# A two-block transformer on one core: queue orders of the second mixer, tile 1's last copy at a feed-forward's end, and the output in halves

## The reference, cut to what matters

```python
def swiglu_2(h, w_in, w_out):
    g, u = jnp.split(h @ w_in, 2, axis=-1)
    return (jax.nn.silu(g) * u) @ w_out

def token_mixer(h, ...):                       # second block
    aq, ak, av, mq, mk, mv, mo, mg = jnp.split(h @ w_in, cuts, axis=-1)
    attn_out = merge_heads(dilated_attention_mixture(rotary(aq) * 64 ** -0.5, rotary(ak), av))   # 8 heads of 64
    qk = jax.nn.silu(conv5(concat([mq, mk])) + conv_b)      # 5 taps along the tokens, each channel for itself
    mq, mk = jnp.split(qk, 2, axis=-1)                      # 4 heads of 128
    mk = mk * 128 ** -0.5
    gates = mg + gate_bias
    cell = mlstm(mq, mk, mv, gates[0], gates[1]) + flip(mlstm(flip(mq), flip(mk), ...))   # two directions
    # in each: num / maximum(abs(den), exp(-m)), num and den linear in mk
    cell = cell * rsqrt(mean(cell ** 2) + eps)
    mlstm_out = sigmoid(mo) * (merge_heads(cell) * mlstm_norm_gain)
    return concat([attn_out, mlstm_out]) @ w_out

# second block: x = x + factor * rms_norm(h, gain) after each part
```

## Time and profile before

| | us |
|---|---|
| median of 3 runs (lowest to highest) | 2189.46 (2186.26 to 2193.22) |
| the three runs | 2189.46, 2186.26, 2193.22 |
| the profiled execution's own time | 2188.38 |
| its span, first to last instruction | 2186.6 |
| mean granted TensorE clock | 0.997 of full speed |

### The profile page before, as it was taken

One profiled execution on the slowest core, in us unless ns is written; L12 is line 12 of the kernel. 1 busy time (PEld: TensorE's weight loads), 2 busy tenths in 40 slices (PEclk: granted clock), 3 DMA queues, 4 the chain that ended last, 5 costly groups with the idle time before them and its releaser, 6 DMA issues.

```text
span 2186.6 us, 27850 instructions
## 1 busy us (share of the span) xinstructions
PE 2150.4 (98%) x10882; PEld 1807.2 (83%) x10882; DVE 1314.8 (60%) x1826; ACT 1070.1 (49%) x1540; POOL 70.9 (3%) x107
## 2 busy tenths in 40 slices
PE   8999999999999999999999999999999999999998
PEld 7888999888888899988878888778888888867887
DVE  5556866555655676655575566575556556667554
ACT  6444544444444454444454456544445445654443
POOL 0000010000000001000000000010000000001000
PEclk9999999999999999999999999999999999999999
DMA  7766654666666675476666656336666666534663
GB/s 244 236 185 185 204 180 139 218 192 186 199 188 188 180 211 178 137 230 187 188 195 191 185 163 188 99 101 216 191 187 199 187 188 177 164 98 144 186 188 99
DMA packets 313654, 393.65 MB, mean 180 GB/s; under 512 B 17796, under 2 KB 272020, under 8 KB 313524
## 3 DMA queue, kind: packets, MB, share of 16 engines
q1 hardware_dynamic: 308832, 375.52, 56.9%
q0 software_dynamic: 4528, 16.29, 2.4%
q10 hardware_dynamic: 164, 0.06, 0.0%
HBM read 390.75 MB, written 1.05 MB: 179 GB/s over the span
## 4 chain that ended last, share of the span: by engine, by line
PE 91%; DVE 3%; ACT 2%; issue 2%; DMA 1%; POOL 0%; SPq 0%; POOLq 0%; DVEq 0%; ACTq 0%
PE bank L307 25%; PE bank L309 24%; PE bank L308 24%; PE bank L301 4%; PE bank L303 4%; PE bank L302 4%; PE bank L433 2%; DMA stage<-in_mix_w_in 1%; ACT w_hi L284 1%; PE bank L446 1%; DVE w_lo L291 1%; PE bank L1375 1%; PE bank L909 1%; PE bank L1396 1%; DVE scratch L1807 0%
## 5 line engine op out<-in xcount | busy, mean ns | idle before, releaser
L291 DVE TENSOR_TENSOR w_lo<-stage,w_hi 128x1024 fp32r<-128x1024 f32 x711 | 865.7, 1224 | 666.1 <-ACT w_hi L284 665.1
L284 ACT ACTIVATE w_hi<-stage 128x1024 fp32r<-128x1024 f32 x711 | 748.4, 1059 | 727.3 <-PE bank L309 585.5
L307 PE MATMUL bank<-w_hi,xt_hi 128*128 128x512 f32 x1760 | 699.9, 398 | 3.7 <-DVE scratch L1718 3.1
L309 PE MATMUL bank<-w_hi,xt_lo 128*128 128x512 f32 x1760 | 687.2, 390 | 0.0
L308 PE MATMUL bank<-w_lo,xt_hi 128*128 128x512 f32 x1760 | 686.1, 390 | 0.0
L307 PEld LDWEIGHTS bank<-w_hi,xt_hi 128*128 128x128 f32 x1760 | 330.9, 188 | 73.2 <-DVE scratch L1718 3.9
L309 PEld LDWEIGHTS bank<-w_hi,xt_lo 128*128 128x128 f32 x1760 | 330.6, 188 | 70.8
L308 PEld LDWEIGHTS bank<-w_lo,xt_hi 128*128 128x128 f32 x1760 | 331.3, 188 | 64.4
L307 PE MATMUL bank<-w_hi,mt_hi 128*128 128x512 f32 x768 | 304.1, 396 | 4.0 <-DVE mt_lo L1865 1.9
L309 PE MATMUL bank<-w_hi,mt_lo 128*128 128x512 f32 x768 | 299.8, 390 | 0.0
L308 PE MATMUL bank<-w_lo,mt_hi 128*128 128x512 f32 x768 | 299.0, 389 | 0.0
(11 more groups left out here) (264 smaller groups left out, 1422.4 us busy)
## 6 DMA issues: line engine op xcount, KB each, us to landing
stage<-in_ffn_w SPq DMA_DIRECT2D x352, 256.0 KB, 3.3
stage<-in_ffn_w_in SPq DMA_DIRECT2D x352, 256.0 KB, 3.2
stage<-in_ffn_w SPq DMA_DIRECT2D x88, 512.0 KB, 3.6
stage<-in_ffn_w_out SPq DMA_DIRECT2D x88, 512.0 KB, 3.6
stage<-in_w_in SPq DMA_DIRECT2D x80, 512.0 KB, 4.4
stage<-in_mix_w_in SPq DMA_DIRECT2D x56, 512.0 KB, 4.2
stage<-in_w_out SPq DMA_DIRECT2D x16, 512.0 KB, 4.5
stage<-in_mix_w_out SPq DMA_DIRECT2D x16, 512.0 KB, 3.4
```

The costliest lines, as they stand in the source:

```text
L284: act.activation(w_hi[:, u % RING, :], stage[:, u % STAGED, :], ACT.Copy).then_inc(S["hi_ready"], 1)
L291: dve.tensor_tensor(w_lo[:, u % RING, :], stage[:, u % STAGED, :], f32(w_hi[:, u % RING, :]), ALU.subtract).then_inc(S["lo_ready"], 1)
L307: pe.matmul(o, m_hi, hi, start=first, stop=False)
L309: return pe.matmul(o, m_lo, hi, start=False, stop=last)
```

## The change

Seven edits.

1. End of an FFN: ACT's `act_h` of tile 1's last values comes ahead of `hi_upto(b + n + 5)`.
2. Mixer 2, gates: ACT's `hi_upto(b + 18)` comes behind the copy of g_feat.
3. Mixer 2, convolution: `conv_in(3)` in DVE's list for head 4 in place of head 5.
4. Mixer 2, Silu: ACT does it, and then the copy g_cols, ahead of `hi_upto(b + 36)` instead of behind. The scaling of the keys is left out; DVE multiplies g_em (the floor of the denominator) by 128 ** 0.5 instead, and m_pair(0) waits for the Silu itself.
5. Head loop, ACT: at h = 0 the exponentials come ahead of `hi_upto(b + 38)`, later the roundings come behind the squares.
6. Head loop, DVE: the order args, gated_cells(h - 2), cells(h - 1), weights(h) becomes args, weights(h), cells(h - 1), gated_cells(h - 2).
7. Output: the last stage's update of x in two halves of 512 columns for each tile, and four transfers of 256 KB in place of two of 512 KB.

```diff
@@ -541,8 +541,8 @@
                         act_h(act, s, 1, i)
             act_norm_sq(act, s, 0)
             act_silu(act, s, 1, STEPS - 1)
+            act_h(act, s, 1, STEPS - 1)
             hi_upto(act, b + n + 5)
-            act_h(act, s, 1, STEPS - 1)
             if s + 1 < len(STAGES):
                 hi_upto(act, b + n + 6)
                 act_xt(act, s + 1, 0)
@@ -609,7 +609,9 @@
         def x_at(s, t, h):
-            return 4 * s + 2 * t + h + 1 if s < BLOCK2 else 4 * BLOCK2 + 2 * (s - BLOCK2) + t + 1
+            if s < BLOCK2:
+                return 4 * s + 2 * t + h + 1
+            return 4 * BLOCK2 + 2 * (s - BLOCK2) + (t if s + 1 < len(STAGES) else 2 * t + h) + 1
         def x_done(s, t):
             return x_at(s, t, 1)
@@ -710,8 +712,10 @@
             else:
                 dve.wait_ge(S["post_scaled"], 2 * post_at(s, t))
                 dve.wait_ge(S["post_rstd"], post_at(s, t))
-                dve.scalar_tensor_tensor(x[:, t, :], r[:, t, :], rstd[:, t:t + 1], x[:, t, :], ALU.mult, ALU.add)\
-                   .then_inc(S["x_ready"], 1)
+                w = D if s + 1 < len(STAGES) else D // 2
+                for c in range(0, D, w):
+                    dve.scalar_tensor_tensor(x[:, t, c:c + w], r[:, t, c:c + w], rstd[:, t:t + 1], x[:, t, c:c + w],
+                                             ALU.mult, ALU.add).then_inc(S["x_ready"], 1)
         def act_pre_sq(act, s, t):
             act.wait_ge(S["x_ready"], x_done(s - 1, t))
@@ -1442,7 +1446,7 @@
                 if h == 0:
                     pe.wait_ge(S["mo_out"], at("mo_out", L, 2))
-                    pe.wait_ge(S["k_scaled"], at("k_scaled", L))
+                    pe.wait_ge(S["conv_silu"], at("conv_silu", L))
                 else:
                     pe_hold(pe, S["m_p"], at("m_p", L, 4 * h))
                 for j in range(NT):
@@ -1536,10 +1540,10 @@
             hi_upto(act, b + 17)
             act.wait_ge(S["used"], b + 8)
             aqk_tile(1)
-            hi_upto(act, b + 18)
             act.activation(half2, scale2[:, :], ACT.Copy, scale=0.5).then_inc(S["srow_out"], 1)
             act.wait_ge(S["gates"], at("gates", L))
             act.activation(g_feat, bank[0:NG, 2, 0:T], ACT.Copy).then_inc(S["gates_out"], 1)
+            hi_upto(act, b + 18)
             act.wait_ge(S["srow"], at("srow", L))
             act.activation(s_row, bank[:, 3, 0:T], ACT.Copy).then_inc(S["srow_out"], 1)
             hi_upto(act, b + 19)
@@ -1578,12 +1582,12 @@
                            .then_inc(S["a_exp"], 1)
                     if h in (1, 2, 4, 5):
                         conv_first((0, 0, 1, 1, 2, 3)[h])
-            hi_upto(act, b + 36)
+            act.wait_ge(S["conv"], at("conv", L))
+            act.activation(conv_y[:, :, :], conv_y[:, :, :], ACT.Silu).then_inc(S["conv_silu"], 1)
             act.wait_ge(S["g_cols_turned"], at("g_cols_turned", L))
             act.activation(g_cols, bank[:, 0, 0:64].rearrange("p (m d i r) -> p m d i r", m=2, d=2, i=NT), ACT.Copy)\
                .then_inc(S["g_cols"], 1)
-            act.wait_ge(S["conv"], at("conv", L))
-            act.activation(conv_y[:, :, :], conv_y[:, :, :], ACT.Silu).then_inc(S["conv_silu"], 1)
+            hi_upto(act, b + 36)
             def mvo_tile(t):
                 act.activation(va[:, t, :, 0:P], group[:, t, 0:512].rearrange("p (h e) -> p h e", h=H), ACT.Identity,
@@ -1616,13 +1620,15 @@
                                    accum_out=ss[:, 2 * h + i:2 * h + i + 1]).then_inc(S["m_ss"], 1)
             for h in range(H):
-                hi_upto(act, b + 38 + h)
                 for d in range(2):
                     act.wait_ge(S["m_arg"], at("m_arg", L, 4 * h + 2 * d + 2))
                     act.activation(m_w[:, d, :], m_e[:, d, :], ACT.Exp).then_inc(S["m_exp"], 1)
+                if h == 0:
+                    hi_upto(act, b + 38)
                 if h:
                     forward(h - 1)
                     squares(h - 1)
+                    hi_upto(act, b + 38 + h)
             forward(H - 1)
             act.wait_ge(S["mg_turned"], at("mg_turned", L, 2))
             act.activation(mt_hi[:, 4:6, :], merged[:, 0:2, :], ACT.Copy).then_inc(S["m_hi"], 1)
@@ -1752,8 +1758,8 @@
                 if h == 4:
                     conv_in(2)
                     conv_taps(1, (3, 4))
+                    conv_in(3)
                 if h == 5:
-                    conv_in(3)
                     conv_taps(2, (1, 2))
                 if h == 6:
                     conv_taps(2, (3, 4))
@@ -1771,9 +1777,6 @@
                                         bank[:, 2 + i, :].rearrange("p (h c) -> p h c", h=AH),
                                         a_rs[:, :, i:i + 1].broadcast_to([P, AH, DH]), ALU.mult)
             ins.then_inc(S["a_out"], 1)
-            dve.wait_ge(S["conv_silu"], at("conv_silu", L))
-            dve.tensor_scalar(conv_y[:, 4:8, :], conv_y[:, 4:8, :], float(P) ** -0.5, None, ALU.mult)\
-               .then_inc(S["k_scaled"], 1)
             lo_upto(dve, base + 36)
             for t in range(NT):
                 dve.wait_ge(S["m_hi"], at("m_hi", L, t + 1))
@@ -1845,12 +1848,14 @@
             dve.scalar_tensor_tensor(gm, gm, 1.0, rows[:, 1, 0:512].unsqueeze(1).broadcast_to([P, NT, 512]),
                                      ALU.add, ALU.mult).then_inc(S["mo_gain"], 1)
             dve.wait_ge(S["g_em"], at("g_em", L))
+            dve.tensor_scalar(g_em, g_em, float(P) ** 0.5, None, ALU.mult).then_inc(S["k_scaled"], 1)
+            dve.wait_ge(S["k_scaled"], at("k_scaled", L))
             for h in range(1, H):
                 args(h)
+                weights(h)
+                cells(h - 1)
                 if h >= 2:
                     gated_cells(h - 2)
-                cells(h - 1)
-                weights(h)
                 cell_var(h - 1)
                 lo_upto(dve, base + 36 + h)
             gated_cells(H - 2)
@@ -1906,9 +1911,11 @@
                 else:
                     sp_ffn(sp, s, A["ffn_w_in_2"][L, j], A["ffn_w_out_2"][L, j])
             for t in range(NT):
-                sp.wait_ge(S["x_ready"], x_done(len(STAGES) - 1, t))
-                sp.dma_start(out[0, t * P:(t + 1) * P, :], x[:, t, :]).then_inc(S["x_out"], 16)
-            sp.wait_ge(S["x_out"], 32)
+                for h in range(2):
+                    c = slice(h * 512, (h + 1) * 512)
+                    sp.wait_ge(S["x_ready"], x_at(len(STAGES) - 1, t, h))
+                    sp.dma_start(out[0, t * P:(t + 1) * P, c], x[:, t, c]).then_inc(S["x_out"], 16)
+            sp.wait_ge(S["x_out"], 64)
         @block.gpsimd
         def _(pool):
```

## The result

The changed kernel takes 2169.8 (median of 4 runs, 2169.18 to 2171.8) against 2188.39 for the kernel before on the same chip (4 runs, 2186.26 to 2193.22). The ratio is 0.9914, 95% interval 0.9898 to 0.9929: 0.9% faster. Forecast were 2174 and a range of 2170 to 2181, so the direction was right and the time lies 0.2 under the range (run once more beside later experiments, the same kernel took 2170.18, e9). The profiled execution took 2169.18 where that of before took 2188.38, and the spans differ by the same 19.2. The sum in the prediction was 14.9. The question is where the other 4.3 come from.

What follows compares the result with a forecast made beforehand. It took PE, busy 98%, as the bound, leaving stream gaps, granted clock and the tail. Terms of 1.1, 3.1, 0.3, 2.4, 3.2, 1.8, 2.7 and 0.3 summed to 14.9 off 2188.4; with 1.1 for a median, 2174, range 2170 to 2181.

Steps and rivals of the forecast that it cites:

- What bounds the kernel: Whole span: PE is busy 98%, so only gaps in its stream, its granted clock and the tail can move the time.
- Gates, conv, Silu: Second mixer: removed PE waits give 1.1 (gates), 3.1 (conv_in(3) earlier) and net 0.3 (Silu first, new wait 0.5 a layer).
- Exponentials ahead of two roundings: Second mixer's head loop: six m_pair waits of 5.6 go, new lateness loses 3.2, net gain 2.4 (0 to 4.5).
- rival B: Head loop: weights(0) still late, so the idle, the low clock and some overlap stay lost: 2181; chance 0.10.
- DVE becomes the slower of the two: Head loop: DVE needs 6.7 a head against PE's 6.3, part of a loss of 1.6 per layer.
- DVE late: Head loop: two heads leave DVE 0.8 late, so m_out(3) waits 2.4 in all.
- 0.16 a gap: PE's stream: each wait also loses 0.16 of matmul overlap; 17 gaps fewer give 2.7 (0 to 3.5).
- The clock: Layer 0's second mixer: the 1.2 GHz stretch behind the idle 2.10 at m_pair(1) goes, gaining 3.2.
- Rival A: Second mixer: idle of 2.4 and 1.8 before L1478 brings new low-clock stretches: one gives 2177, two 2180; chance 0.25.
- C: Rival, slower: the Silu ahead of the roundings starves PE at n = 30, giving 2177 to 2196; chance 0.03.
- D: Rival, no change: the gaps turn out hidden by other waits of the same length, 2186; chance 0.05.
- Output: Kernel's end: last update and stores in halves gain 0.3 (between -0.5 and +0.8).

Runs made afterwards that it cites:

- e9: The changed kernel, unedited, run again beside e6 and e7: 2170.18 (4 runs), ratio 0.9911.
- e5: The changed kernel with one more DVE product, its result unused, behind the w_lo of heads 1 and 2: 2172.72 (one run).
- e3: The changed kernel with DVE's old head-loop order back (gated cells and cells ahead of weights): 2171.86, ratio 0.9917.
- e1: The kernel before with the FFN edit alone (tile 1's last turned values copied ahead of the two roundings): 2185.53 against 2191.44, ratio 0.9977.
- e2: The changed kernel with head 0's two roundings ahead of the exponentials again: 2176.52, ratio 0.9942.
- e10: The kernel before with only head 0's exponentials moved ahead of the two roundings: 2181.94, ratio 0.996.
- e11: The kernel before with the conv edit alone (conv_in(3) one head earlier): 2185.09 against 2191.73, ratio 0.9977.
- e7: The changed kernel with e6's edit, w_lo up to b+34 moved behind the attention output, and head 2's denominators ahead of weights(3): 2166.16, ratio 0.989.
- e6: The changed kernel with the head loop's last DVE w_lo moved behind gated_cells(3): 2168.22, ratio 0.9901.

## Why the prediction was right, and where it was not

*What bounds the kernel.* Right: of the 19.2, all but the 0.5 at the end are gaps in PE's stream or its granted clock, and they lie at the waits in the earlier trace rows.

*Gates, conv, Silu.* Right in mechanism and nearly in size: 1.3, 3.7 and 0.8 (1.9 less 1.1) against 1.4, 3.4 and 0.3. conv alone on before gives the same as in the whole. The gates edit was neither tried alone nor undone; its 1.3 is read from the wait that went. The new wait of L1442 is 0.4 a layer, not 0.5, so the load and the Silu are the 3.2 that I gave them: in after too the Silu starts 1.30 behind the load's start. The Trainium skill, ScalarE: Activation LUTs, section "What ACT_TABLE_LOAD costs", has a drain of about 1.4 behind the load; as an estimate from it L1442 would wait 1.4 longer. The trace disagrees: it waits 0.40.

*Exponentials ahead of two roundings.* Right for m_pair(1), (2), (3): 6.5 against 6.6 with the overlap. The margin of 0.1 to 0.2 was enough; rival B fell.

*DVE becomes the slower of the two: wrong, and the step that failed.* The prediction summed DVE's head as args to weights 2.6, cells 1.75, "wait for the squares 0.97 (1440.24 to 1441.21)", variance 0.16 and w_lo 1.22, or 6.7. The interval of 0.97 is no wait. DVE's timeline of before, head 3:

```profile
1440.16 1.14 DVE L1807 TENSOR_TENSOR scratch<-scratch,bank 128x256 f32<-128x256 f32 x4
```

It lies in that interval: DVE was doing the weights, which the sum already had in its first term. ACT squares the cells meanwhile, and in after the variance comes 0.50 behind the cells (in heads 2 and 3 the gated cells, 0.60, which the sum leaves out, fill that time). DVE's timeline of after, one head:

```profile
1412.31 1.39 DVE L1799 SCALAR_TENSOR_TENSOR hidden<-bank,small,const 128x256 f32<-128x256 f32 x4 [1.18 <-PE bank L1456]
1413.64 1.28 DVE L1810 TENSOR_TENSOR scratch<-scratch,bank 128x256 f32<-128x256 f32 x4
...
1415.97 0.61 DVE L1827 SCALAR_TENSOR_TENSOR scratch<-bank,small,scratch 128x128 f32<-128x128 f32 x2 [0.52 <-ACT scratch L1613]
...
1417.09 0.17 DVE L1833 TENSOR_SCALAR var<-ss 128x2 f32<-128x2 f32 x1 [0.50 <-ACT scratch L1619]
1417.16 1.22 DVE L291 TENSOR_TENSOR w_lo<-stage,w_hi 128x1024 fp32r<-128x1024 f32 x1
```

From 1412.31 to 1418.38 is 6.07. PE's pairs start at 1410.04, 1416.33 and 1422.55, 6.29 and 6.22 apart. DVE is the faster, so nothing accumulates. What is left of that part is the order itself: args(3) at 1424.67, m_out(3) at 1429.09, 4.42 apart where I had 4.45. The 0.3 for it was right; the 0.8 for "DVE late" was not there. L1482 waits 1.33 and not 1.8, since it hung on the same interval: the variance comes 0.35 behind the start of m_out(3) (1429.44, 1429.09), where I had 0.9. The 0.8 and the 0.5 that were not there make 1.3 a layer. e5 shows that the reasoning from a slow DVE to a late m_out(3) was sound, and e3 that the order gains instead of losing.

*The restart.* The term "0.16 a gap" was mis-sized for gaps in the stream of 512 columns: 0.24 at the FFN ends (e1), which is 0.7 of the 4.3. At m_pair, whose matmuls have 256 columns, the steps less the waits are (6.5 - 5.6) / 6 = 0.15, as counted. With the 2.8 above that leaves 0.8, spread over seven lines of the table, none over 0.3 off; I did not follow it further. Over all places the steps exceed the waits by 3.7, where I had 2.7 and at most 3.5.

*The range.* It was said to take in the bounds of the parts. Their upper ends add up to 19.4, which gives its lower end of 2170, but their lower ends add up to 0.5, far outside it on the slow side. Two parts went past their own upper ends: the head loop gave 5.2 (5.6 less 0.4) where I allowed 4.5, and the restarts 3.7 where I allowed 3.5. Both misses have one sign, and so the time came to lie just below the range.

*The clock.* The 3.2 in layer 0 was right, and the guess from the spread of before's three runs fits what came since: runs of none, one and two such stretches, about 3 apart (e9). e2 and e10 show what brings it, the idle ahead of m_pair(1); e1 shows that it can also begin ahead of that idle, behind the 0.71 at m_pair(0), whose wait the change removes as well. A run of before at the median of many loses it in both layers, as far as its clock tells: beside e9 the medians lie 20.9 apart (2191.12, 2170.18), 2.3 more than the 18.6 of the first comparison.

*Rival A* was not seen in after: 1.53 and 1.33 of idle left the clock at 1.00. It is a real mechanism all the same: at 2.34 it came in one layer of two (e5), at 1.61 in both (e2). Why 1.61 at m_pair(1) brings it and 1.53 at m_out(3), with 1.33 behind it, does not stays open; the work around the two places differs, and no run here varied that alone. *C* and *D* are out: L1442 waits 0.4, and the three edits tried alone (e1, e11, e10) each gave their own gain.

*Output.* 0.5 against 0.3, within its bounds; the landing fell by 0.6. The Trainium skill, DMA: Bandwidth & Descriptors, section "Anatomy of one DMA — SWDGE (gpsimd) path", gives a fixed and a size term for transfers on GpSimd's path, while these stores are issued by SP; as an estimate from it the 256 KB are worth 0.6. The trace agrees on that difference, though not on the whole (2.0 where the two terms give 2.6).

## What to carry to other kernels

When you cost a loop in a new order, mark each interval between two rows as busy or idle first: what looks like a wait for another engine may be this engine's own next job, and moving that job moves the interval away. Price a stall of a streaming TensorE as its idle and the restart (here 0.24 for 512 columns), and look in the granted clock for what a longer stall leaves behind. And try the small neighbours of a reordering too: moving two DVE roundings of weights and one group of tiny products gained another 4.0 here (e7).

## What the runs showed of the hardware that was not expected

- The same idle of 2.14 in one program left the granted clock at 1.00 in layer 0 and brought 1.2 GHz in layer 1 (e11); an idle of 1.61 was enough in both layers of e2, and 0.71 in one layer of e1. Such a stretch cost 1.6 (e2) to 3.2 (before), and nothing where a wait stood behind it (e1).
- A tiny POOL instruction took 1.59 beside a DVE product of two SBUF operands, ending 0.54 behind it, and 0.69 alone (e6).
- A store of 256 KB landed in 2.0, one of 512 KB in 2.6 (after, before).
